# Hybrid encoder trunk on one core: output-projection slots, low-part splits and one gate stage moved inside the head-pair stage

## The reference

```python
for i in range(DEPTH):
    u = _rms_norm(h, norm_mix[i])
    z_rw, z_gd, z_ml = jnp.split(u @ w_in[i], [RW_COLS, RW_COLS + GD_COLS], axis=-1)
    y = jnp.concatenate([y_rw, y_gd, y_ml], axis=-1)      # the three mixes of the three parts
    h = h + y @ w_out[i]
    up = _dwconv_centred(_rms_norm(h, norm_ffn[i]) @ w_up[i], ffn_conv_w[i]) + ffn_conv_b[i]
    gate, val = jnp.split(up, 2, axis=-1)
    h = h + (jax.nn.silu(gate) * val) @ w_down[i]
    h = h + jax.nn.sigmoid(_rms_norm(h, norm_ple[i]) @ w_ple_gate[i]) * (p[i] @ w_ple_proj[i])
```

```python
L = jnp.where(strict, jnp.einsum("...id,...jd->...ij", kb, k) * decay, 0.0)
sol = lax.linalg.triangular_solve(eye + L, rhs, left_side=True, lower=True, unit_diagonal=True)
w = jnp.exp(log_w - m_t[..., None]) * jnp.einsum("...td,...sd->...ts", q_c, k_c)     # mLSTM
```

## Time and profile before

| | |
|---|---|
| median of 3 runs | 3601.46 us (3598.64 to 3605.71) |
| profiled execution | 3605.71 us, of which the span is 3604.0 us |
| TensorE busy (matmul / weight load) | 3306.6 us (92%) / 2923.3 us (81%) |
| VectorE / ScalarE / GpSimd busy | 2227.8 (62%) / 1622.0 (45%) / 437.0 us (12%) |
| the chain that ended last | PE 76%, DVE 12%, issue 4%, ACT 3%, DVEq 3%, POOL 1% |
| DMA | 477.13 MB, 132 GB/s |
| GpSimd in the pair stage | 42 low-part splits, 2.36 us each; 24 additions to H, 2.37 us each |

### The profile page before, as it was taken

How to read it: one execution, slowest core, us unless ns; L and a number is a source line. 1 busy time by engine, 2 the same in 40 slices (tenths; PEclk the granted TensorE clock), 3 DMA queues, 4 the chain that set the end, 5 groups by cost and what they waited for, 6 DMA issues and landing times.

```text
span 3604.0 us, 55774 instructions
## 1 busy us (share of the span) xinstructions
PE 3306.6 (92%) x19450; PEld 2923.3 (81%) x19450; DVE 2227.8 (62%) x3615; ACT 1622.0 (45%) x2429; POOL 437.0 (12%) x263
## 2 busy tenths in 40 slices
PE   6999778888899999999989997788889999999998
PEld 6999667777788888887789996787777888888876
DVE  4565666567677777544455655656776777775444
ACT  5444323344555555444354443233445555554443
POOL 2000000244022222100000000002440222220000
PEclk9999788799899999999999997888999999999999
DMA  5566000111466666555555660001115666656554
GB/s 173 155 175 186 22 0 0 52 53 48 124 192 186 186 190 195 188 187 177 165 158 162 181 174 1 0 1 58 48 47 160 190 189 189 187 182 199 187 194 134
DMA packets 263066, 477.13 MB, mean 132 GB/s; under 512 B 16988, under 2 KB 80280, under 8 KB 261720
## 3 DMA queue, kind: packets, MB, share of 16 engines
q1 hardware_dynamic: 262872, 474.63, 43.0%
HBM read 472.47 MB, written 2.10 MB: 132 GB/s over the span
## 4 chain that ended last, share of the span: by engine, by line
PE 76%; DVE 12%; issue 4%; ACT 3%; DVEq 3%; DMA 1%; POOL 1%; ACTq 0%; POOLq 0%; SPq 0%
PE ps L505 75%; DVE Z L1405 1%; DVE scores L1663 1%; DVE wlo L1382 1%; PE ps L509 1%; DVE XS L1438 1%; DMA ring<-in_w_ple_gate_dram 1%; ACT whi L1016 1%; ACT L1016 1%; DVE scores L1814 0%; DVEq L1407 0%; DMA ring<-in_w_in_dram 0%; ACT Z L1016 0%; POOL wlo L441 0%; DVE heads L1467 0%
## 5 line engine op out<-in xcount | busy, mean ns | idle before, releaser
L1382 DVE TENSOR_TENSOR wlo<-ring,whi 128x1024 fp32r<-128x1024 f32 (+4 forms) x902 | 1130.5, 1267 | 835.0 <-ACT whi L1016 833.2
L505 PE MATMUL ps<-upair,whi 128*128 128x512 f32 (+1 forms) x5248 | 1421.5, 342 | 19.8 <-DVE wlo L1382 17.9
L1016 ACT ACTIVATE whi<-ring 128x1024 fp32r<-128x1024 f32 (+4 forms) x944 | 943.7, 1004 | 1049.9 <-PE ps L505 969.2
L505 PE MATMUL ps<-upair,wlo 128*128 128x256 f32 x4032 | 1134.9, 281 | 0.0
L505 PEld LDWEIGHTS ps<-upair,whi 128*128 128x128 f32 x5248 | 910.4, 190 | 138.6 <-DVE wlo L1382 20.3
L505 PEld LDWEIGHTS ps<-upair,wlo 128*128 128x128 f32 x4032 | 768.2, 191 | 0.0
L505 PE MATMUL ps<-whi,upair 128*128 128x390 f32 (+2 forms) x1280 | 362.7, 362 | 2.0 <-DVE wlo L1382 2.0
L505 PE MATMUL ps<-whi,ghi 128*128 128x512 f32 x704 | 278.5, 396 | 2.3 <-DVE wlo L1382 2.3
L505 PE MATMUL ps<-whi,glo 128*128 128x512 f32 x704 | 277.8, 395 | 0.0
L505 PE MATMUL ps<-wlo,ghi 128*128 128x512 f32 x704 | 277.7, 395 | 0.0
L505 PEld LDWEIGHTS ps<-whi,upair 128*128 128x128 f32 x1280 | 237.2, 188 | 24.3 <-DVE wlo L1382 3.2
(11 more groups left out here) (282 smaller groups left out, 3690.2 us busy)
## 6 DMA issues: line engine op xcount, KB each, us to landing
ring<-in_w_up_dram SPq DMA_DIRECT2D x352, 512.0 KB, 3.9
ring<-in_w_down_dram SPq DMA_DIRECT2D x176, 512.0 KB, 4.5
ring<-in_w_in_dram SPq DMA_DIRECT2D x128, 384.0 KB, 3.6
ring<-in_w_out_dram SPq DMA_DIRECT2D x64, 512.0 KB, 3.8
ring<-in_w_ple_gate_dram SPq DMA_DIRECT2D x64, 512.0 KB, 4.5
ring<-in_w_in_dram SPq DMA_DIRECT2D x64, 390.0 KB, 3.2
ring<-in_w_in_dram SPq DMA_DIRECT2D x48, 512.0 KB, 4.4
ring<-in_w_in_dram SPq DMA_DIRECT2D x32, 396.0 KB, 4.0
```

What stands on the lines that cost most here:

```text
L505: return pe.matmul(o_, a, b, start=start, stop=stop, skip_group_check=True)
L1016: return act.activation(o_, i_, f, **kw)
L1382: v.tensor_tensor(wlo[:, slot % RING, :, 0:w], ring[:, slot % RING, :, 0:w], whi[:, slot % RING, :, 0:w].bitcast(F32), SUB).then_inc(S["lo ...
```

## The change

It moves work within the pair stage on four engines; no arithmetic is added or taken away.

- TensorE: slot 2 leaves level 2. Slot 2 is now in level 4, slot 3 in level 5, slot 4 behind the inverse, and 5, 6 and 7 at the end of the pair.
- GpSimd: the wait for `inv_tn1` is gone; after the four decay masks (L460) it goes straight on with slot 2 and both leftover additions, then slots 3 and 4, one addition, slot 5. The mLSTM masks stand ahead of slot 6 instead of behind it.
- ScalarE: the high part of slot 6 and partial sum 1 are handled behind level 4, slot 7 behind the inverse, slot 8 (the next pair's slot 0) where partial sum 2 was copied out, and partial sum 2 behind slot 9.
- VectorE: mLSTM stage 0, and the wait for `gd_ssq` ahead of it, leave the head of the pair; stage 0 now stands between level 0 and level 1.

```diff
--- before.py
+++ after.py
@@ -459,23 +459,21 @@
                             pool.wait_ge(S["gd_d"], pool.snap(n * 2) + (2 * d + j + 1))
                             pool.tensor_tensor(scores[d][:, j, :, :], scores[d][:, j, :, :], bmid(mask[d][:], 4),
                                                ALU.mult).then_inc(S["gd_dm"], 1)
-                    pool.wait_ge(S["inv_tn1"], pool.snap(L * (2 * (RC + GP)) + (i * 2 + 2 * RC)) + 2)
                     if i:
+                        split_lo(sg, SL_OUT + 2)
                         add_partial(ng, -2)
-                        split_lo(sg, SL_OUT + 2)
+                        add_partial(ng, -1)
                     split_lo(sg, SL_OUT + 3)
-                    if i:
-                        add_partial(ng, -1)
                     split_lo(sg, SL_OUT + 4)
                     add_partial(ng, 0)
                     split_lo(sg, SL_OUT + 5)
-                    split_lo(sg, SL_OUT + 6)
                     for d in range(2):
                         pool.wait_ge(S["ml_d"], n + (d + 1))
                         dg = ml_diag(d)
                         for h in range(2):
                             pool.tensor_tensor(dg[h], dg[h], bmid(incl[d][:], 2), ALU.mult)
                         pool.drain().then_inc(S["ml_dm"], 1)
+                    split_lo(sg, SL_OUT + 6)
                     split_lo(sg, SL_OUT + 7)
                     add_partial(ng, 1)
                 pool.wait_ge(S["gd_done"], L * GP + GP)
@@ -886,9 +884,9 @@
                         pe.wait_ge(S["gd_ktc"], n + 1)
 
                     invert(m2, lambda d, j: scores[d][:, 2, j, :], {lv: lambda lv=lv: ml_pair(n, n2, lv) for lv in (1, 2, 4, 5)},
-                           {(0, "x", 1): lambda: out_slot(i, 1), (0, "t", 0): before_t, (2, "t", 0): lambda: out_slot(i, 2),
-                            (LEV - 2, "t", 0): lambda: out_slot(i, 3), (LEV - 1, "t", 0): lambda: out_slot(i, 4)})
-                    out_slot(i, 5)
+                           {(0, "x", 1): lambda: out_slot(i, 1), (0, "t", 0): before_t, (LEV - 2, "t", 0): lambda: out_slot(i, 2),
+                            (LEV - 1, "t", 0): lambda: out_slot(i, 3)})
+                    out_slot(i, 4)
                     for d in range(2):
                         F = FIRST[d]
                         inverted(m2, d)
@@ -927,7 +925,7 @@
                             j = 2 * h + B
                             last = mm(ps[4 * d + 3][:, j * P:(j + 1) * P], scores[d][:, 3, j, :], KBt[d][:, h, :], True, True)
                         last.then_inc(S["gd_y"], 1)
-                    for s in range(6, OUT_SLOTS):
+                    for s in range(5, OUT_SLOTS):
                         out_slot(i, s)
 
                 pe.wait_ge(S["wo_evac"], L * (GP * NO) + GP * NO)
@@ -1265,22 +1263,21 @@
                     split_out(sg, lg, 5)
                     def between_levels(lv):
                         ml_pair(n2, lv)
-                        if lv == 2:
+                        if lv == LEV - 2:
                             split_out(sg, lg, 6)
-                        if lv == LEV - 2:
                             partial_out(ng, sg, 1)
-                            split_out(sg, lg, 7)
                     t1(m2, between_levels)
-                    split_out(sg, lg, 8)
+                    split_out(sg, lg, 7)
                     for src, dst, lo, done in (("gd_u", ufg, 0, "gd_uf"), ("gd_us", KBt, T, "gd_usc")):
                         if src == "gd_us":
-                            partial_out(ng, sg, 2)
+                            split_out(sg, lg, 8)
                             act.wait_ge(S["ml_ss"], n + 1)
                             rsqrt(st[:, 2, :], st[:, 1, :], 1.0 / P, epsb[:, 0:1]).then_inc(S["ml_rstd"], 1)
                         for d in range(2):
                             act.wait_ge(S[src], n2 + (d + 1))
                             a(mono(dst[d][:, :, :], 2), ps[4 * d][:, lo:lo + T], ACT.Copy).then_inc(S[done], 1)
                     split_out(sg, lg, 9)
+                    partial_out(ng, sg, 2)
                     act.wait_ge(S["gd_ss"], n + 1)
                     rsqrt(st[:, 2, :], st[:, 1, :], 1.0 / P, epsb[:, 0:1]).then_inc(S["gd_rstd"], 1)
                     split_out(sg, lg, 10)
@@ -1826,8 +1823,6 @@
                         for d in range(2):
                             masked_scores(d, 1)
 
-                    v.wait_ge(S["gd_ssq"], n + 1)
-                    ml_pair(i, n, n2, 0)
                     exponents(0, 0)
                     exponents(0, 1)
                     v.wait_ge(S["gd_rn"], n + 1)
@@ -1845,7 +1840,7 @@
                         v.drain()
                         v.tensor_tensor(scores[d][:, 2, :, :], scores[d][:, 2, :, :], bmid(ident[:, :], 4), ADD)
                         invert_start(d, scores[d][:, 2, :, :])
-                    invert(m2, lambda lv: lv and ml_pair(i, n, n2, lv), products)
+                    invert(m2, lambda lv: ml_pair(i, n, n2, lv), products)
 
                     v.wait_ge(S["gd_vtc"], n + 1)
                     v.wait_ge(S["gd_ktc"], n + 1)
```

## The result

The changed kernel takes 3662.14 us (median of 4 runs, 3654.43 to 3671.57) against 3602.41 us (3598.64 to 3605.71): a ratio of 1.0168, with a 95% interval of 1.0144 to 1.0193. It is slower, as forecast, but by some 60 us instead of 21, and so outside the range. The profiled execution took 3663.07 us with a span of 3661.3, which is 57.3 more than before.

| pair | 1 | 2 | 3 | 1 | 2 | 3 | sum | half clock in them |
|---|---|---|---|---|---|---|---|---|
| before | 91.3 | 84.6 | 88.4 | 91.3 | 84.6 | 88.4 | 528.6 | 64.5 |
| after | 91.9 | 95.2 | 102.8 | 99.0 | 95.4 | 103.0 | 587.3 | 133.8 |

A forecast was written before the change was run, and what follows sets the result against it. Pairs were taken as bound by tight TensorE and VectorE alternation, about 520 of 3604 us. Per layer, +1.1 for the first pair and +4.6 for each other made 10.3, two layers +20.6: 3622 us, range 3594 to 3638.

The forecast's parts named there:

- head of the pair: Start of pairs 2 and 3: third slot hidden in TensorE's idle time, L1836 starts earlier; -1.6 us a pair.
- the wait for `inv_tn1` goes: Start of the inverse: direction 1's two-input VectorE instructions wait for GpSimd's stream; +2.6 us, bounds 0 and +4.5.
- stage 0 between levels 0 and 1: VectorE's copies there wait for GpSimd; +4.55 us with their own work, bounds +0.75 and +6.75.
- level 2 without a slot: Level 2 of the inverse: t can start when the first `XS` is there; -1.5 us.
- masks ahead of split 6 (level 4): Level 4: VectorE's 2.44 us wait for masks goes, and TensorE's 2.06 idle with it; -2.05 us.
- end of the inverse: Stage 5's L1789 waits about 2.2 us for a GpSimd split, stage 4 adds 0.4; +2.6 us, bounds 0.4 and 3.6.
- copies are not held up: Rival: stage 0 between levels costs only 0.75 us, a pair +0.8, six pairs +5.4, 3607 us; chance 0.20.
- the sum's tacit term for the clock: Half clock was weighed only at the pair's head, where the -1.6 us might shrink to about -0.3; none priced elsewhere.
- The stream hurts more: Rival: stage 0 waits for two whole GpSimd instructions, L1857 for one; pair +7.8, total +35, 3637 us; chance 0.14.
- The first pair: First pair of each layer: GpSimd is through before stage 0, which costs 0.75; the head gives -1.3; +1.1 us.

The follow-up runs named there:

- undo_wait: The changed kernel with GpSimd's wait for `inv_tn1` put back ahead of its slot splits; ratio 1.0143 to the kernel before.
- hold: The changed kernel with GpSimd's splits of pairs 2 and 3 held until VectorE has ended stage 0; ratio 1.0069 to the kernel before.
- Filler: The changed kernel with nine unread TensorE products added ahead of level 1 in pairs 2 and 3; 3657.69 us, ratio 1.0114 to the kernel before.
- delay: The kernel before with eight unread VectorE reductions added between levels 0 and 1 in pairs 2 and 3; ratio 1.0090.
- masks_first: The kernel before with only GpSimd's mLSTM masks moved ahead of split 6; 3586.16 us against 3611.62, ratio 0.9914.
- late_partial: The changed kernel with ScalarE's reciprocal root of the gated delta norm ahead of the copy of partial sum 2; ratio 1.0114 to the kernel before.
- undo_both: The changed kernel with stage 0 back at the head and GpSimd's wait for `inv_tn1` put back; ratio 1.0019 to the kernel before.
- undo_stage0: The changed kernel with mLSTM stage 0 and its wait for the squared norms back at the head; 3636.83 us, ratio 1.0057 to the kernel before.

## Why the prediction was right in direction and wrong in size

By its own steps, in the second pair of layer 1 (after minus before, read at the ends of VectorE's instructions from the pair's start; forecast in brackets):

| step | measured | forecast |
|---|---|---|
| head of the pair | -1.4 | -1.6 |
| the wait for `inv_tn1` goes | +2.6 | +2.6 |
| stage 0 between levels 0 and 1 | +5.7 | +4.55 |
| from level 1's `XS` to level 2's, at half clock | +4.7 | not priced |
| level 2 without a slot | -1.3 | -1.5 |
| masks ahead of split 6 (level 4) | -3.0 | -2.05 |
| end of the inverse | +2.0 | +2.6 |
| state update behind it | +1.3 | not priced |
| pair | +10.6 | +4.6 |

(The first two are split by the milestone of undo_wait.)

*What held.* The mechanisms that were forecast did: the idle time at the head and the wait for the masks went, the two-input instructions met the stream at the forecast price, the copies of stage 0 were held up too, and L1786 (L1789 before) waited 2.0 us in stage 4 and 1.7 in stage 5, against 2.2 forecast for stage 5. The rule of the Trainium skill on copies ("SBUF — State Buffer", section "Who interferes with whom") that no row of before could show agrees with the trace: 2.43 us against 0.286 for a copy, and 2.46 for a TENSOR_SCALAR (L1753, first pair of layer 2). Rival "copies are not held up" is refuted by hold against the changed kernel.

*The step that failed* is the sum's tacit term for the clock. The prediction weighed half clock only at the head, where it saw idle time go, and not where it put idle time: it wrote "+4.55" for stage 0, which leaves TensorE without work for some 5 us, and let level 1 to 3 run at their old pace. The trace of before had a stretch at 0.66 behind 2.75 us of idle time, so the question could have been asked. Filler shows the clock's part with the change in place (4.5 us a pair), delay shows it with no port in dispute. In the six pairs half clock grew by 69.3 us; not all of it is lost, as other engines set the pace in part of it. What is lost is 4.7 us from level 1 to level 2 in each second and third pair, 19 us in four pairs, which is half of the 38 us by which the forecast for the six pairs was short. The other half is several smaller terms, and here follow the ones that the rows show.

*The mis-sized terms.* Stage 0 was 1.1 us dearer in pair 2 and 1.4 in pair 3, inside its bounds; it waited for two whole instructions of GpSimd (2.43 and 2.42 us), not for one. That, and the stretched L1852, are the conditions of the rival "The stream hurts more", so for the ports that rival describes what happened better than the forecast does. In pair 3 the difference at level 1's `XS` is +6.9 from the pair's start, as in pair 2. The masks were worth 3.0 in level 4 instead of 2.05 (masks_first shows the same 3.0 by itself), on the good side. The state update's 1.3 us were not traced to a cause. In pair 3 of a layer the end of the inverse takes 3.9 us more instead of 2.0, and 1.7 us more come behind the last output product, where ScalarE's copies of partial sum 2 now stand: a cost that the sum does not have, and of which late_partial gives back 1.0. The first pair took +0.6 in layer 1, near the forecast of 1.1, but +7.7 in layer 2: there L1753 started 0.03 us behind a GpSimd split and waited for it, stage 0 took 3.18 us, and half clock followed. The forecast's "GpSimd [...] is through before stage 0" thus holds, to within 0.1 us, in one of two layers, which was luck, and in filler in none. Summed: 0.6 + 10.6 + 14.4 + 7.7 + 10.8 + 14.6 = 58.7 against 20.6.

*What the change is made of.* The parts don't add up. The masks alone gain 17.0; with the slots they lose 16.0; with stage 0 moved too 55.2; with all parts 58.7. Whichever part makes GpSimd's stream meet VectorE pays, and the first to do so pays most: without the wait the pairs take 22.7 us more on top of masks_first, 12.3 on top of undo_both and 3.5 on top of undo_wait; the move of stage 0 costs 71.1, 39.2 and 30.4 us on top of masks_first, undo_both and undo_stage0. The forecast took the terms one by one in the order of time and came close on most. Undo_both shows that the new slots and GpSimd's new order, which I had at -1.6 - 1.5 + 2.6 in pairs 2 and 3, cost 33.0 us over masks_first in six pairs once stage 0 stands at the head. The rows show parts of it: stage 0 held up at the head, ScalarE waiting for the later additions, and the dearer end of pair 3. None of these is in the sum, and the shares were not measured apart.

## What to carry to other kernels

Price a new idle time of TensorE twice: its own length, and the stretch at half clock that may follow, here 6.8 to 17.1 us long around 5.2 to 7.3 us of idle time, and in delay and filler worth 2 to 7 us. Before moving a VectorE step, lay it against GpSimd's timeline: a copy between SBUF tiles, of whatever size, can wait for the end of GpSimd's instruction, while instructions with an operand in PSUM (L1435 at 0.65 us beside an addition, second pair) and reductions kept their length. And try the parts of a change apart: here one of them was a gain that the others hid, 0.5% by the pairs and 0.6 to 1.2% by the times.

## What the runs showed of the hardware that was not expected

- A copy of 6x2 elements waited 2.30 us beside GpSimd, and one of 128x24 took 2.32 us: the wait doesn't shrink with the copy. Not every copy waits: in the second pair of the changed kernel two of stage 0's instructions waited over 2 us, and L1753 right ahead of them took 0.28.
- GpSimd pays as well: in the changed kernel the three instructions around the stretched L1423 (a split from 761.68 and two additions) took 2.81 to 2.84 us instead of 2.36.
- The same program shows two lengths of its first pair, 91.9 and 99.0 us in one execution, and stage 0 shows how little decides: in layer 1 it starts at 689.15, 0.03 us before GpSimd's last split ends, and takes 1.0 us; in layer 2 L1753 starts at 2495.14, 0.03 us behind the start of a split, and stage 0 takes 3.18 us.
- Stretches at half clock can last far longer than the idle time that they come with, and their length varies: 13.7 us with 5.17 us idle in the second pair of the changed kernel and 17.1 with 6.43 in the third, but 6.8 and 13.7 with 5.64 in delay, and 17.1 and 6.8 with 7.25 in hold.
